# Ends of four token-tile stages reordered, and the first feed-forward unit moved into the stage before it, in a two-block transformer kernel

## The reference

```python
def first_block(...):      # hyena + rwkv mixer, then 16 experts
    x = x + m_lat[2] * rmsnorm(mixed, p['norm1_post'])
    h2 = rmsnorm(x, p['norm2_pre']) * (1.0 + m_lat[4]) + m_lat[3]
    x = x + m_lat[5] * rmsnorm(expert_choice_moe(h2, p), p['norm2_post'])
def second_block(...):     # layer 0: sparse attention; layer 1: s5 state space with a gated product
    for i in range(DEPTH_2):
        h = rms_norm(x, norm_mix[i]) * (1.0 + sc_m) + sh_m
        y = dsa_attention(h, ...) if i % N_MIXERS == 0 else s5_mixer(h, ...)
        x = x + g_m * y
        h = rms_norm(x, norm_ffn[i]) * (1.0 + sc_f) + sh_f
        x = x + g_f * conv_ffn(h, ffn_w_up[i], ffn_conv_w[i], ffn_conv_b[i], ffn_w_down[i])
def conv_ffn(h, w_up, conv_w, conv_b, w_down):   # D_FF = 2816
    up = depthwise_causal_conv3(h @ w_up) + conv_b
    val, gate = jnp.split(up, 2, axis=-1)
    return (jax.nn.silu(gate) * val) @ w_down
```

## Time and profile before

| what | value |
|---|---|
| median of 3 runs | 3699.44 us (3698.45 to 3700.58) |
| the profiled execution's own time | 3696.78 us |
| its span in the trace | 3695.0 us |
| mean granted TensorE clock | 0.967 of full speed |
| PE busy | 3364.4 us, 91% |
| DVE busy | 1154.8 us, 31% |
| ACT busy | 599.8 us, 16% |
| ends of the stages: A, B, C, D (last PE record) | 1106.9, 2128.1, 2525.3, 3226.3 us |

### The profile page before, as it was taken

How to read it: one execution, slowest core, us unless ns; L and a number is a source line. 1 busy time by engine, 2 the same in 40 slices (tenths; PEclk the granted TensorE clock), 3 DMA queues, 4 the chain that set the end, 5 groups by cost and what they waited for, 6 DMA issues and landing times. The chain is left out here.

```text
span 3695.0 us, 48197 instructions
## 1 busy us (share of the span) xinstructions
PE 3364.4 (91%) x21265; PEld 1676.5 (45%) x21265; DVE 1154.8 (31%) x1987; ACT 599.8 (16%) x1188; POOL 8.1 (0%) x40
## 2 busy tenths in 40 slices
PE   6978999998987888988998899999999978999998
PEld 3557887444443333332332444454444444444443
DVE  2255655443022000000001236634665042222211
ACT  2134222110020000000000212232211012211100
POOL 0000000000000000000000000000000000000000
PEclk9989999899988999999999999999999988999999
DMA  6134445211128999999999321102433244222220
GB/s 240 46 122 163 163 147 179 87 35 57 68 97 344 430 430 430 430 428 430 427 428 430 144 96 46 46 15 72 157 126 128 76 120 172 69 68 68 76 90 34
DMA packets 197141, 666.66 MB, mean 180 GB/s; under 512 B 31048, under 2 KB 96060, under 8 KB 170693
## 3 DMA queue, kind: packets, MB, share of 16 engines
q1 hardware_dynamic: 195944, 663.21, 46.0%
q10 hardware_dynamic: 989, 0.36, 0.0%
HBM read 638.88 MB, written 22.31 MB: 179 GB/s over the span
## 5 line engine op out<-in xcount | busy, mean ns | idle before, releaser
L2758 PE MATMUL banks<-h_T,weight_ring 128*128 128x512 f32 x1408 | 614.3, 597 | 5.8 <-PEq L90 5.8
L2758 PEld LDWEIGHTS banks<-h_T,weight_ring 128*128 128x128 f32 x1408 | 268.0, 192 | 338.8 <-issue 338.7
L2060 PE MATMUL banks<-weight_ring,xe_T 128*64 128x512 f32 x1312 | 295.4, 597 | 42.5 <-DMA weight_ring<-in_exp_w 40.4
L2770 PE MATMUL banks<-weight_ring,ffn_act 128*128 128x512 f32 x704 | 302.5, 592 | 0.0
L2856 DVE SCALAR_TENSOR_TENSOR conv<-banks,cols,conv 128x510 f32<-128x510 f32 (+1 forms) x176 | 131.8, 749 | 342.8 <-ACT conv L2826 338.1
L2770 PEld LDWEIGHTS banks<-weight_ring,ffn_act 128*128 128x128 f32 x704 | 133.8, 190 | 168.4 <-issue 168.4
L2060 PEld LDWEIGHTS banks<-weight_ring,xe_T 128*64 128x64 f32 x1312 | 90.0, 137 | 235.2 <-issue 158.8
L2076 PE MATMUL banks<-weight_ring,hid_T 128*64 128x512 f32 x656 | 146.8, 596 | 10.6 <-DMA weight_ring<-in_exp_w 10.6
L2826 ACT ACTIVATE conv<-banks,cols 128x512 f32<-128x512 f32 x88 | 63.7, 773 | 504.8 <-PE banks L2758 504.8
L2381 PE MATMUL banks<-h_T,weight_ring 128*128 128x512 f32 x320 | 142.0, 597 | 0.0
L2060 PE MATMUL banks<-h_T,xe_T 128*64 128x512 f32 x464 | 105.4, 596 | 17.7 <-DMA h_T<-in_exp_w 17.7
(11 more groups left out here) (587 smaller groups left out, 4100.5 us busy)
## 6 DMA issues: line engine op xcount, KB each, us to landing
weight_ring<-in_exp_w SPq DMA_DIRECT2D x123, 2048.0 KB, 15.7
h_T<-in_exp_w SPq DMA_DIRECT2D x41, 2048.0 KB, 15.7
weight_ring<-in_ada_w SPq DMA_DIRECT2D x24, 2048.0 KB, 8.8
weight_ring<-in_ffn_w_up SPq DMA_DIRECT2D x44, 1024.0 KB, 6.7
expert_out<-in_exp_w SPq DMA_DIRECT2D x19, 2048.0 KB, 19.1
weight_ring<-in_mod_w SPq DMA_DIRECT2D x12, 2048.0 KB, 8.6
weight_ring<-in_ffn_w_down SPq DMA_DIRECT2D x10, 2048.0 KB, 7.8
spare<-in_exp_w SPq DMA_DIRECT2D x9, 2048.0 KB, 20.5
```

The source lines that it names most:

```text
L2060: mm = pe.matmul(k.ps[64 * half:64 * half + 64, 2 * c + b % 2, :], R.rows[:, e // 2 % 2, kt, (e % 2) * CAP:(e % 2 + 1) * CAP], w[:, r, 512 ...
L2758: mm = pe.matmul(k.ps[:, b + c, :], w[:, c, kt, m * P:m * P + P], hT[:, kt, :], start=kt == 0, stop=kt == 7)
L2770: return pe.matmul(k.ps[:, 2 * t + n, :], out[:, kt, t * P:t * P + P], src[:, n * 512:n * 512 + 512], start=kt == 0, stop=kt == FF_T - 1)
```

## The change

In all five stages ACT first runs one square root of a constant, so that its table is loaded before it is needed. Within the tails the shift of an earlier tile now comes ahead of root and scaling of the tile, and in B and C (`lag` = 1) it is that of tile t-1. In B, and with a first product of the next stage also in C and D, the turn of the next tile is put into the middle of the product that follows. In C and D that product is new: `first_unit`, unit 0 of the feed-forward stage behind, done in two halves of 256 columns (tiles 0 and 1, then 2 and 3). `conv_ffn` leaves out the products of unit 0 and only takes its banks. In D the turns of tiles 0 and 1 stand in the middle of the products of tiles 2 and 3. The side job's first steps move one or two units later, and `dve_columns` and `dve_powers` both stand behind unit 3's convolution.

```diff
 def to_residual(...)
+    lag = 2 if norm and from_ring else 1
...
-                        if tail and t >= 2:
-                            T.pe_turn(pe, t - 2, banks(t - 2))
+                        if tail and from_ring and t >= lag:
+                            turn(t - lag)
+                        if tail and not from_ring and t == 2:
+                            turn(0)
...
-            if tail:
+            if tail and not from_ring:
+                for t in range(LT):
+                    then(t, (lambda: turn(t + 1)) if t + 1 < LT else None)
+            elif tail and norm:
                 for t in range(LT - 2, LT):
-                    if follow:
-                        then(t - 2)
-                    T.pe_turn(pe, t, banks(t))
-            if follow:
+                    then(t - 2)
+                    turn(t)
                 for t in range(LT - 2, LT):
                     then(t)
+            elif tail:
+                then(1, lambda: turn(3))
+                then(3)
...
         def _(act):
+            if norm or tail:
+                act.activation(ss[:, 1, 0:1], k.misc[:, 6:7], ACT.Sqrt)
...
                 if tail:
+                    if t >= lag:
+                        T.act_shift(act, t - lag, banks(t - lag))
                     T.act_root(act, t)
-                    if t >= 2:
-                        T.act_shift(act, t - 2, banks(t - 2))
...
+def first_unit(k, n, banks):
+
+    def products(pe, t, middle):
+        two = slice((t - 1) * P, (t + 1) * P)
+        k.ring.wait(pe, n)
+        w = k.ring.chunk(n).rearrange("p (c k n) -> p c k n", c=2, k=8)
+        for c in range(2):
+            for kt in range(8):
+                pe.matmul(k.ps[:, banks[c], two], w[:, c, kt, 0:P], k.hT[:, kt, two], start=kt == 0, stop=kt == 7)
+            if c == 0 and middle:
+                middle()
+
+    return products
...
 def conv_ffn(k, hT, layer, side):
+                    if i == 0:
+                        pe.sem_inc(products, 1)
+                    else:
+                        for c in range(2):
+                            for kt in range(8):
+                                mm = pe.matmul(k.ps[:, b + c, :], w[:, c, kt, m * P:m * P + P], hT[:, kt, :], start=kt == 0, stop=kt == 7)
+                        mm.then_inc(products, 1)
-                    if side and i == 0:
+                    if side and i == 2:
                         side.pe_c(pe, banks)
-                    if side and i == 2:
+                    if side and i == 3:
                         side.pe_cols(pe, banks)
...
-                    if side and i == 0:
+                    if side and i == 1:
                         side.dve_angles(dve, side_link)
-                    if side and i == 1:
+                    if side and i == 2:
                         side.dve_factors(dve, side_link)
-                    if side and i == 2:
+                    if side and i == 3:
                         side.dve_columns(dve, side_link, banks)
-                    if side and i == 3:
                         side.dve_powers(dve, side_link)
...
 def s5_glu(k, g, gain, tail):
                         for kt in range(DT):
                             mm = pe.matmul(k.ps[:, 4 * c + t, :], g[:, kt, t * P:t * P + P], w[:, kt, :], start=kt == 0, stop=kt == 7)
+                            if n and c and t >= 2 and kt == 3:
+                                T.pe_turn(pe, t - 2, banks(t - 2))
...
+            then(1, lambda: T.pe_turn(pe, 2, banks(2)))
+            T.pe_turn(pe, 3, banks(3))
+            then(3)
...
                     m = 4 * n + t
+                    if n and t >= 2:
+                        T.act_shift(act, t - 2, banks(t - 2))
...
                     dve.sem_inc(updated, 1)
-                    T.dve_normed(dve, t)
                     if t >= 2:
                         T.dve_shift(dve, t - 2, banks(t - 2))
+                    T.dve_normed(dve, t)
```

More of the change, by code:

```diff
@@ L1845, in add_base, with turn, then @@
                 return mm
+            def turn(t):
+                T.pe_turn(pe, t, banks(t))
+            def then(t, middle=None):
+                pe.wait_ge(T.shifted_a, t + 1)
+                pe.wait_ge(T.shifted_v, t + 1)
+                if load and t == 0:
+                    pe.wait_ge(follow_landed, 16)
+                follow(pe, t, middle)
             kt = 0
@@ L1895, in _ @@
                 if tail:
+                    if t >= lag:
+                        T.act_shift(act, t - lag, banks(t - lag))
                     T.act_root(act, t)
-                    if t >= 2:
-                        T.act_shift(act, t - 2, banks(t - 2))
             if tail:
-                for t in range(LT - 2, LT):
+                for t in range(LT - lag, LT):
                     T.act_shift(act, t, banks(t))
@@ L1920, in _ @@
                 if tail:
+                    if t >= lag:
+                        T.dve_shift(dve, t - lag, banks(t - lag))
                     T.dve_normed(dve, t)
-                    if t >= 2:
-                        T.dve_shift(dve, t - 2, banks(t - 2))
             if tail:
-                for t in range(LT - 2, LT):
+                for t in range(LT - lag, LT):
                     T.dve_shift(dve, t, banks(t))
@@ L2249, in first_layer, with logits @@
                 wr = cw.enter_context(sbuf(nc, "router_w", [P, DT, N_EXP], F32))
-                def logits(pe, t):
+                def logits(pe, t, middle):
                     for kt in range(DT):
@@ L2290, in first_values @@
 def first_values(k):
-    def products(pe, t):
+    def products(pe, t, middle):
         if t == 0:
@@ L2301, in products @@
             pe.matmul(k.ps[:, 2 * t + 1, 0:IDX_HEADS], h, ww[:, kt, 64:72], start=kt == 0, stop=kt == 7)
+            if kt == 3 and middle:
+                middle()
+    return products
+def first_unit(k, n, banks):
+    def products(pe, t, middle):
+        two = slice((t - 1) * P, (t + 1) * P)
[5 more added lines that the diff above has]
+            if c == 0 and middle:
+                middle()
     return products
@@ L2695, in sparse_attention @@
             attend(k, qT, kT, v, mask, qscale, oT)
-        to_residual(k, lambda kt: oT[:, kt, :], None, [4, 4], 2, False, tail=(k.scales[:, 0, 8:16], k.mod2[:, 0, 24:32], k.hT))
+        to_residual(k, lambda kt: oT[:, kt, :], None, [4, 4], 2, False, tail=(k.scales[:, 0, 8:16], k.mod2[:, 0, 24:32], k.hT),
+                    follow=first_unit(k, 2, (0, 1)))
 def conv_ffn(k, hT, layer, side):
@@ L2703, in conv_ffn @@
     banks = k.ps[:, 6:8, :]
+    bank = lambda i, c: 4 * c if i == 0 and not side else 2 * (i % depth) + c
     gain, kts = 3 + 2 * layer, [4, 4, 4, 4, 4, 2]
@@ L2755, in _ @@
                         pe.wait_ge(conved, i - depth + 1)
-                    for c in range(2):
-                        for kt in range(8):
-                            mm = pe.matmul(k.ps[:, b + c, :], w[:, c, kt, m * P:m * P + P], hT[:, kt, :], start=kt == 0, stop=kt == 7)
-                    mm.then_inc(products, 1)
-                    if side and i == 0:
+                    if i == 2 and not side:
+                        pe.wait_ge(conved, 1)
+                    if i == 0:
[6 more added lines that the diff above has]
+                    if side and i == 2:
                         side.pe_c(pe, banks)
-                    if side and i == 2:
+                    if side and i == 3:
                         side.pe_cols(pe, banks)
@@ L2831, in _ @@
                     if side and i == 1:
+                        side.act_exp(act)
+                    if side and i == 2:
                         side.act_c(act, banks)
@@ L2849, in _ @@
                 for i in range(FF_T):
-                    b = 2 * (i % depth)
                     dve.wait_ge(middle, i + 1)
@@ L3339, in keep @@
                                    k.ps[:, 6 + h, :].rearrange("p (i k) -> p i k", i=STEP), ACT.Copy).then_inc(kept, 1)
+            act.activation(rstd[:, 1, 0:1], k.misc[:, 6:7], ACT.Sqrt)
             act.wait_ge(grouped, 1)
@@ L3444, in _, with then @@
                             mm = pe.matmul(k.ps[:, 4 * c + t, :], g[:, kt, t * P:t * P + P], w[:, kt, :], start=kt == 0, stop=kt == 7)
+                            if n and c and t >= 2 and kt == 3:
+                                T.pe_turn(pe, t - 2, banks(t - 2))
                         mm.then_inc(products, 1)
-                        if n and c and t >= 2:
-                            T.pe_turn(pe, t - 2, banks(t - 2))
-            for t in range(LT - 2, LT):
-                T.pe_turn(pe, t, banks(t))
+            follow = first_unit(k, 4, banks(0))
+            def then(t, middle=None):
+                pe.wait_ge(T.shifted_a, t + 1)
+                pe.wait_ge(T.shifted_v, t + 1)
+                follow(pe, t, middle)
+            then(1, lambda: T.pe_turn(pe, 2, banks(2)))
+            T.pe_turn(pe, 3, banks(3))
+            then(3)
         @block.scalar
```

16 lines of the change are left out of this document (3 added, 13 removed).

## The result

The changed kernel takes 3672.69 us (median of 4 runs, 3670.85 to 3674.84), the kernel before 3698.94 (4 runs, 3693.51 to 3700.58). The ratio is 0.9932, 95% interval 0.9918 to 0.9945, so 25 us less, with 20 to 30 as bounds. Forecast were 3676 us (3668 to 3686) and 23.3 us less. The profiled execution took 3671.68 us around a span of 3669.9.

What follows compares the result with a forecast made beforehand. PE's products were taken as the bound nearly everywhere, so edits pay where PE idles or runs at the lower clock. Gains 2.5+11.1+7.4+0.3+2.0 = 23.3 us off the 3699.44 median gave 3676 us, range 3668 to 3686.

Steps and rivals of the forecast that it cites:

- A: Stage A: DVE's shift of tile 1 no longer waits for the last root and scaling, `logits` starts earlier; gain 2.5 us.
- up to 1 us more: Stage A: extra gain if the clock fell later than in the profile read for the prediction.
- B: Stage B: early table load, values straight behind the products, no restart from long idle; gain 11.1 us, least 8.5.
- the slow restart: Stage B: PE's slow first work after long idle time, priced at 2.6 us, would no longer occur.
- S: Stage S: root's table loaded early, so the root need not wait for the load; gain 0.3 us.
- D: Ahead of the second feed-forward stage: PE idles 5.7 us, restart costs 2.6, unit 1 starts earlier; gain 2.0 us.
- C: Ahead of the first feed-forward stage: unit 0 in halves gains 8.5 us, less 1.1 for the side job; 7.4 us.
- The late convolution of unit 4: First feed-forward stage: DVE starts this convolution 2.0 us late, slack 0.97, so PE waits 1.1 us once behind unit 5.
- the restarts decide more: Rival: clock may stay up at D's wait (+2.6 us) and B's first products meet a higher clock; 3671 us, chance 0.15.
- Restarts at the lower clock in C and D's last wait: Rival: waiting plus turning of tile 3 lowers the clock, costing 3.25 us each in C and D; 3682 us, chance 0.15.
- The moved unit gains nothing: Rival: something else holds unit 1 at its old time, C and D give nothing; 3685.5 us, chance 0.07.
- Slower: Rival: B's values run at granted clock 0.50 throughout because of turns between products; 3711 us, chance 0.03.

Runs made afterwards that it cites:

- d_shift_first: Changed kernel with, in D, DVE's shift of tile t-2 ahead of its operations on tile t's gated product: 3667.32 us, ratio to before 0.993.
- best: Changed kernel with D's shifts earlier, unit 0's second pair there as single tiles, side job's first turn inside unit 6: 3663.21 us, ratio to before 0.9912.
- powers_late: Changed kernel with the side job's powers on DVE one unit later, behind unit 4's operations: 3681.74 us, a single run.
- b_only: Kernel before with the edits of stage B alone: ratio to before 0.9971 (0.996 to 0.9982).

## Why the prediction was right

The mechanism held in every stage; its steps one by one. **A** gained 2.5 us, as forecast; in three executions (d_shift_first, best, powers_late) it was 3.6, the "up to 1 us more" of the prediction: the clock fell later there, and `logits` of tile 1 took 2.2 to 2.3 us, not 3.56. **B** gained 11.17 us for 11.1, with no wait left. The values start 16.8 us behind B's first product, as forecast, and the slow restart is gone. That both profiles began B with slow records is chance: in six executions with the new order of B its start was fast, and B 1.7 us shorter. **S** gained 0.35 us for 0.3. **D**: the wait 5.55 for 5.7, the last shifts 1.60 for 1.6, the restart at a granted clock of 0.50; unit 1 about 1.6 us earlier for 2.0 (29.2 less 26.7 in the table, less the 0.87 by which a turn now delays tile 3's products); of the difference 0.15 us is a meeting of 1.05 for 0.9.

**C** is the term that was mis-sized: 8.1 less 1.4 = 6.7 us, forecast 8.5 less 1.1 = 7.4. Of the 8.5 us, 3.25 were the slow unit 0 of before (32 records in 17.02 us). In b_only, where C is the old one, these records took 15.42 us, so 1.6 us of the term hang on the one execution from which it was read, and the table has 81.1 us there. Up to the turn of tile 3 the rows stand where they were put, 62.1 us behind C's first product. Then 48 records take 10.53 for 10.32 us, and the meeting 1.05 for 0.9. The turn behind unit 5 waits 1.09 us by the row, but what PE loses is 1.3, since the idle time counts from the modelled end of the last record, 0.17 us behind the next start. Its cause was put half wrong. The late convolution of unit 4 was right, as was its price. But "DVE has `dve_columns` and `dve_powers` behind one unit" is not the reason: powers_late has them apart and waits 6.01 us. What counts is DVE's whole work up to the deadline and that it doesn't stand idle in between.

Of the rivals *the restarts decide more* (3671) came true in part. In D the clock fell and the first 16 records were slow in both profiles of the changed kernel (5.97 and 5.83 us), as forecast. But B met a higher clock in the second one (52.3 for 54.0 us), and the second measurement has its median at 3670.87. The others did not come true. *Restarts at the lower clock in C and D's last wait* (3682): in C the wait of 0.85 us and the turn behind it left the 48 records of 256 columns at 0.22 us each (10.53 us), full speed, and in D the turn of tile 3 and the wait of 1.60 us left 32 records at 7.17 us. The Trainium skill's statement that transposes don't count as busy the way products do ("TensorE: Matmul & The Clock Gate", "Part 4: PE-mode transpose") had no effect on the time here; these rows don't decide whether it holds. *The moved unit gains nothing*: C's edits alone gain 5.5 us by the runs, and in the changed kernel unit 1 starts 1.05 us behind the last half. *Slower*: the values took 37.2 us with three turns among them, at full speed.

That the time came out within 3.3 us of 3676 is partly luck. The sum was 23.3 us; the stages of the first pair of profiles gave 21.4, those of the second profile of the changed kernel 27.9, and the measured medians 25 to 26. The sum has no term for what the clock does in attention (1.3 us longer in one profile, 0.8 shorter in the other), in the experts (1.0 us between the two), in S and D together (1.6) and at B's start (1.7), nor for the scatter ahead of A (1024.1 to 1033.3 us). These are larger than the errors of its own terms: 0.7 us in C, 0.4 in D, 0.1 in the rest.

## What to carry to other kernels

Follow the wait into the queue of the engine that is waited for. What cost 5.6 us and a restart of 2.2 us in D was the place of four shifts, 1.36 us together, and moving them was worth 7.0 us, as much as the whole of C. When an engine feeds a deadline, look at the sum of its work and at its idle time up to the deadline: here spreading the side job over more units made the wait 4.9 us longer. Work of PE that is moved forward uncovers what was hidden behind it (here 16.4 us of waiting for loads), so what needs those loads must move too.

## What the runs showed of the hardware

The granted clock at a fixed place of the program differs between executions of one kernel: 0.51 and 1.00 over the first 6 us of the scores, 335.8 and 333.7 us for the stage. In this kernel that makes 1 to 2 us in each of A, B and attention, so differences of 2 us between single profiles prove nothing, even three against three. Products of 128 columns in float32 run at 0.11 us a record (7.38 us less the last one's 0.17, over 64), close to half of the 0.22 us at 256 columns, though each of them loads its weights anew. A wait of 5.55 us of PE was followed by slow records that cost 2.2 us, and filling it with 12 records removed this cost.
